# A hybrid decoder block on one core: the z and x projections get the stationary operand swapped

## The reference

```python
def reference(x, ...):                       # x: (1, 256, 2048) float32
    hn = rmsnorm(x, norm_mix_w)
    z, xbc, dt_raw, u, g_a, g_b = split(hn @ w_in)
    xbc = silu(causal_dwconv(xbc, conv_a_w, conv_a_b))     # 4 taps; x: 3072 channels, b and c: 1024 each
    y_a = mamba2(z, xbc, dt_raw) @ w_proj_a                # uses silu(z)
    y_b = s5(u)                                            # 64 groups, complex states
    h = x + (sigmoid(g_a) * y_a + sigmoid(g_b) * y_b) @ w_out
    h = h + conv_glu_ffn(rmsnorm(h))
    return rmsnorm(h)
```

## Time and profile before

| | us |
|---|---|
| runs | 1680.24, 1680.87, 1680.90 |
| median | 1680.87 |
| the profiled execution, its own time | 1680.3 |
| span of that execution | 1678.6 |

### The profile page before, as it was taken

The page is one execution under the profiler, slowest core; times in us unless marked ns, Lnnn a source line. Parts: engine busy times, 40 slices in busy tenths (PEclk is TensorE's granted clock), DMA queues, the critical chain, the costliest instruction groups (busy, mean ns, idle before and its releaser), DMA issues.

```text
span 1678.6 us, 24422 instructions
## 1 busy us (share of the span) xinstructions
PE 1667.1 (99%) x8340; PEld 1395.1 (83%) x8340; DVE 1320.3 (79%) x1685; ACT 962.7 (57%) x1271; POOL 216.4 (13%) x310
## 2 busy tenths in 40 slices
PE   9999999999999999999999999999999999999997
PEld 8888888888788888888888888888888888888886
DVE  7999999999998986545775868888878888845555
ACT  7676676766666667444557755444444444454553
POOL 7843342221000000000000200000000000000001
PEclk9999999999999999999999999999999999999999
DMA  7666766666666566656786577777777777666653
GB/s 254 213 197 199 204 206 200 193 188 190 194 217 231 191 219 189 199 191 201 239 254 232 174 233 241 243 241 244 242 244 241 245 232 248 225 194 195 191 189 123
DMA packets 174569, 358.49 MB, mean 214 GB/s; under 512 B 16880, under 2 KB 39584, under 8 KB 174368
## 3 DMA queue, kind: packets, MB, share of 16 engines
q1 hardware_dynamic: 162528, 338.26, 62.5%
q0 software_dynamic: 11248, 18.37, 4.6%
q10 hardware_dynamic: 720, 0.93, 0.2%
HBM read 335.41 MB, written 15.80 MB: 209 GB/s over the span
## 4 chain that ended last, share of the span: by engine, by line
PE 73%; DVE 2%; issue 0%; ACT 0%; DVEq 0%
PE psum L1822 22%; PE psum L1823 22%; PE psum L1824 22%; PE psum L1783 3%; PE psum L1785 2%; PE psum L1908 1%; DVE wlo L1107 0%; PE psum L1909 0%; DVE vn L1749 0%; PE psum L1933 0%; DVE bc L1303 0%; PE psum L1829 0%; PE psum L1924 0%; DVE dec L1416 0%; PE psum L1982 0%; PE psum L1979 0%
## 5 line engine op out<-in xcount | busy, mean ns | idle before, releaser
L1107 DVE TENSOR_TENSOR wlo<-raw,whi 128x1024 fp32r<-128x1024 f32 x580 | 709.6, 1230 | 321.3 <-ACT whi L666 314.0
L666 ACT ACTIVATE whi<-raw 128x1024 fp32r<-128x1024 f32 x580 | 611.9, 1058 | 577.1 <-PE psum L1824 455.1
L1783 PE MATMUL psum<-act,whi 128*128 128x512 f32 x1088 | 342.5, 396 | 0.0
L1822 PE MATMUL psum<-whi,nw 128*128 128x512 f32 x704 | 274.1, 389 | 0.0
L1824 PE MATMUL psum<-whi,nw 128*128 128x512 f32 x704 | 273.9, 389 | 0.0
L1823 PE MATMUL psum<-wlo,nw 128*128 128x512 f32 x704 | 273.9, 389 | 0.0
L1785 PEld LDWEIGHTS psum<-act,wlo 128*128 128x128 f32 x1088 | 204.4, 188 | 48.3
L1785 PE MATMUL psum<-act,wlo 128*128 128x256 f32 x1088 | 213.7, 278 | 0.0
L1783 PEld LDWEIGHTS psum<-act,whi 128*128 128x128 f32 x1088 | 165.6, 189 | 3.3 <-issue 2.8
L1824 PEld LDWEIGHTS psum<-whi,nw 128*128 128x128 f32 x704 | 132.1, 188 | 27.6
L1822 PEld LDWEIGHTS psum<-whi,nw 128*128 128x128 f32 x704 | 132.1, 188 | 27.3
(11 more groups left out here) (251 smaller groups left out, 2300.3 us busy)
## 6 DMA issues: line engine op xcount, KB each, us to landing
raw<-in_w_up SPq DMA_DIRECT2D x176, 512.0 KB, 4.9
raw<-in_w_zx SPq DMA_DIRECT2D x96, 512.0 KB, 3.7
raw<-in_w_down SPq DMA_DIRECT2D x88, 512.0 KB, 3.8
raw<-in_w_gate SPq DMA_DIRECT2D x64, 512.0 KB, 5.6
raw<-in_w_proj SPq DMA_DIRECT2D x48, 512.0 KB, 4.4
raw<-in_w_bc SPq DMA_DIRECT2D x32, 512.0 KB, 3.7
raw<-in_w_glu SPq DMA_DIRECT2D x32, 512.0 KB, 4.4
raw<-in_w_out SPq DMA_DIRECT2D x32, 512.0 KB, 4.8
```

The source lines that it names most:

```text
L666: fn(whi[:, s, :], raw[:, s, :], ACTF.Copy).then_inc(hi_ready, 1)
L1107: V.tensor_tensor(wlo[:, s, :], raw[:, s, :], whi[:, s, :], ALU.subtract).then_inc(lo_ready, 1)
L1783: mm(psum[:, b + t, :], whi[:, s, cols(t)], x, start=first, stop=False)
L1822: mm(banks[:, t, :], x_hi, high[:, k], start=j == 0 and k == 0, stop=False)
```

## The change

For zx, PE now calls `unit_tokens`: a chunk is 8 units and gives 256 channels of z and 256 of x for all 256 tokens; a turn has two chunks. Weights are loaded with 2 KB pieces in place of 4 KB ones, from the same data. `take_hsum` and `add_halves` are gone for zx. In their place ACT copies a finished chunk to `flat_x` (`zx_blocks`, two instructions, at the start of rounds 0 and 2), SP writes it to DRAM in four DMAs (`zx_write`, behind the load of unit 2 or 10 of the next turn), waits for them and reads it back into `quad_x` (`zx_fetch`, behind the load of unit 3 or 11), and DVE turns it (`zx_turned_back`, four instructions of 128x256, near the end of rounds 1 and 3): two for z into `zblk`, two for x into `cpad`. So x's tap, convolution and silu follow a chunk later than before: chunk 2i at r = 0 of turn i+1, chunk 2i+1 at r = 2. The last two chunks, 10 and 11, are convolved in bc0, next to bc0's own groups; chunk 11 goes through a pad of its own (`last_pad`).

The core of the diff:

```diff
@@ SyncE
+            def zx_write(c):
+                sp.wait_ge(zx_free, c + 1)
+                for q in range(4):
+                    sp.dma_start(blocks_at[:, :, q, :].rearrange("j p x -> p j x"),
+                                 flat_x[32 * q:32 * q + 32, :, :, :, :].rearrange("p j s t b -> p j (s t b)")
+                                 ).then_inc(zx_written, 16)
+            def zx_fetch(c):
+                sp.wait_ge(zx_written, c * 64 + 64)
+                sp.dma_start(quad_x[:, :, :, :, :].rearrange("p q s t b -> p (q s t b)"),
+                             blocks_at.rearrange("j p q x -> (j p) (q x)")).then_inc(zx_read, 16)
+            def zx_moves(turn, j):
+                if j % 8 == 2:
+                    zx_write(turn * 2 + (j // 8 - 2))
+                if j % 8 == 3:
+                    zx_fetch(turn * 2 + (j // 8 - 2))
@@ ScalarE
+            def zx_blocks(c, cc):
+                act.wait_ge(unit_used, c * 8 + (UNIT0["zx"] + 8))
+                if not (isinstance(c, int) and c == 0):
+                    act.wait_ge(zx_written, c * 64)
+                for t in range(2):
+                    ins = fn(flat_x[:, :, :, t, :].rearrange("p j s b -> p s j b"),
+                             chunk_banks("zx", cc)[:, t, :].rearrange("p (s j b) -> p s j b", s=4, j=4), ACTF.Copy)
+                ins.then_inc(zx_free, 1)
...
+            def z_silu(c):
+                fn(zx[:, ds(c * 2, 2), 0, :], zblk[:, :, :], ACTF.Silu).then_inc(z_done, 1)
@@ VectorE
-                elif name == "zx" and r % 2 == 0:
-                    add_halves(zx[:, ds(i * 4 + r, 2), 0, :], g0 + r, i * per)
...
+            def zx_turned_back(c):
+                pad = cpad
+                dve.wait_ge(zx_read, c * 16 + 16)
+                if isinstance(c, int) and c == 11:
+                    pad = last_pad
+                    V.memset(pad[:, :, 0:3], 0.0).then_inc(pad_zeros, 1)
+                if not (isinstance(c, int) and c == 0):
+                    dve.wait_ge(z_done, c)
+                for t in range(2):
+                    V.transpose(zblk[:, :, t * P:t * P + P].rearrange("p s (q b) -> p q s b", q=4),
+                                quad_x[:, :, 0:2, t, :])
+                if not (isinstance(c, int) and c == 0):
+                    dve.wait_ge(x_conv, c)
+                for t in range(2):
+                    ins = V.transpose(pad[:, :, 3 + t * P:3 + t * P + P].rearrange("p s (q b) -> p q s b", q=4),
+                                      quad_x[:, :, 2:4, t, :])
+                ins.then_inc(zx_turned, 1)
@@ VectorE, mixer_turn
-                    if r or start:
+                    if before[0] == "u" or name == "bc" and r:
                         group_sums(*before)
...
-                    group_conv(*before)
+                    if before[0] != "zx":
+                        group_conv(*before)
+                    if chunks and not start and r % 2 == 0:
+                        x_conv_pair(blk * 2 + (r // 2 - 2))
                     s5_scan(tile, last)
...
-                    if r == per - 1 and not last:
+                    if name == "bc" and r == per - 1 and not last:
                         group_sums(name, i, r)
...
                         last_state_sum(blk)
+                    if r == 3 and name == "zx" or r == 1 and chunks and not start:
+                        zx_turned_back(blk * 2 + (r // 2 - 1))
                     lo(3)
@@ TensorE
+            def zx_turn(i, prev):
+                for c in range(2):
+                    for j in range(8):
+                        if prev is None and c == 0:
+                            pe.wait_ge(vlo_ready, j // 2 + 1)
+                        if prev is not None and c == 1 and j == 0:
+                            pe.wait_ge(y5_out, prev + 1)
+                        unit_tokens("zx", c, j, act16, i)
+                        if c == 0 and j == (0 if prev is None else 1):
+                            s5_drive(i, prev is None)
+                            if prev is not None:
+                                pe.wait_ge(zx_free, i * 2)
+                                s5_products(prev, YS5)
```

More of the change, by code:

```diff
@@ L353, in _, with zx_units @@
                     sp.dma_start(craw[:, :, :, :], a["s5_c"]).then_inc(c_in, 16)
+                if name == "zx":
+                    w = a["w_zx"].rearrange("(c g q) p (h n) -> c q h p g n", g=2, q=quads, h=2)
+                    def zx_units(i):
+                        for j in range(4 * quads):
+                            n, c, q, half = UNIT0[name] + j, j // (2 * quads), j % (2 * quads) // 2, j % 2
+                            sp.wait_ge(lo_ready, i * (4 * quads) + (n - RING + 1))
+                            sp.dma_start(raw[:, n % RING, :].rearrange("p (g n) -> p g n", g=2),
+                                         w[ds(i * 2 + c, 1), q, half].rearrange("o p g n -> (o p) g n")
+                                         ).then_inc(w_in[n % RING], 16)
+                            if not (isinstance(i, int) and i == 0):
+                                zx_moves(i, j)
+                    zx_units(0)
+                    with sp.Fori(1, groups // 4) as i:
+                        zx_units(i)
+                    continue
+                if name == "bc":
+                    for j in range(groups * quads):
+                        n = UNIT0[name] + j
+                        sp.wait_ge(lo_ready, n - RING + 1)
+                        sp.dma_start(raw[:, n % RING, :], a["w_bc"][j]).then_inc(w_in[n % RING], 16)
+                        if j < 16:
+                            zx_moves(6, j)
+                    continue
                 if name == "up":
@@ L762, in sines, with group_tap @@
                    bias=TWO_PI / 4).then_inc(tab_ready, 1)
[L764 to L768, removed]
+            def group_tap(i, r):
+                _, per, quads, u0, g0 = phase("bc")
                 act.wait_ge(sum_ready, i * per + (g0 + r + 1))
@@ L771, in group_tap @@
                 for t in range(2):
[L772 to L775, removed]
+                    to, q = bc[:, ds(i * 4 + r, 1), t, :], i * 8 + (24 + 2 * r + t)
                     ins = fn(to.rearrange("p o n -> p (o n)"), cpad[:, t, 3:3 + L], ACTF.Identity,
@@ L778, in group_tap, with group_silu @@
                 ins.then_inc(tap_ready, 1)
[L780 to L797, removed]
+            def group_silu(i, r):
+                act.wait_ge(conv_done, i * 4 + (r + 1))
+                to = bc[:, ds(i * 4 + r, 1), :, :].rearrange("p o c n -> p (o c) n")
+                fn(to, to, ACTF.Silu).then_inc(xbc_done, 1)
@@ new lines, in zx_blocks, with x_first_tap @@
+            def zx_blocks(c, cc):
[6 more added lines that the diff above has]
+                ins.then_inc(zx_free, 1)
+            def x_first_tap(c):
+                act.wait_ge(zx_turned, c + 1)
+                act.nop(nofuse=True)
+                pad = last_pad if isinstance(c, int) and c == 11 else cpad
+                for t in range(2):
+                    q = c * 2 + t
+                    ins = fn(zx[:, ds(q, 1), 1, :].rearrange("p o n -> p (o n)"), pad[:, t, 3:3 + L], ACTF.Identity,
+                             scale=col("conv_a_w", q * 4 + 3), bias=col("conv_a_b", q))
+                ins.then_inc(x_tap, 1)
@@ L799, in mixer_turn, with x_silu @@
+            def x_silu(c):
+                act.wait_ge(x_conv, c + 1)
+                act.nop(nofuse=True)
+                to = zx[:, ds(c * 2, 2), 1, :]
+                fn(to, to, ACTF.Silu).then_inc(xbc_done, 1)
+            def z_silu(c):
+                fn(zx[:, ds(c * 2, 2), 0, :], zblk[:, :, :], ACTF.Silu).then_inc(z_done, 1)
             def mixer_turn(name, i, blk, prev):
                 _, per, quads, u0, g0 = phase(name)
-                start = prev[0] == "u"
+                first, chunks = prev[0] == "u", name == "zx" or i == 0
@@ L806, in mixer_turn @@
                     before = (name, i, r - 1) if r else prev
+                    behind = blk * 2 + (r // 2 - 2)
                     last = name == "bc" and i == 1 and r == per - 1
-                    group_hsum(*before)
+                    if before[0] != "zx":
+                        group_hsum(*before)
+                    elif r % 2 == 0:
+                        zx_blocks(blk * 2 + (r // 2 - 1), 1 - r // 2)
                     hi(0)
-                    if r >= 2 or not start:
+                    if r >= 2 or not first:
                         act.wait_ge(x5_ready, blk * 4 + (r - 1))
@@ L813, in mixer_turn @@
                     hi(1)
-                    group_tap(*before)
+                    if before[0] == "bc":
+                        group_tap(*before[1:])
+                    if chunks and not first and r % 2 == 0:
+                        x_first_tap(behind)
                     if not last:
@@ L818, in mixer_turn @@
                     hi(2)
-                    group_silu(*before)
+                    if before[0] == "bc":
```

(58 more changed lines are left out.)

16 lines of the change are left out of this document (13 added, 3 removed).

## The result

The changed kernel takes 1699.44 us (median of 1697.13 to 1700.22), the one before 1680.74 beside it: ratio 1.011, 95% interval 1.0092 to 1.0127. It is 18.7 us slower where the forecast was 0.4 us faster, 1680.5 us, and the upper end of its range 1687.0. The profiled execution took 1700.2 us (span 1698.6), so differences read from its trace add up to 20.0 us.

The account below looks back on a forecast made before the run. TensorE bounds the kernel to bc0's drive, VectorE from there to the first gate turn. By VectorE alone, -1.05 - 6.9 + 1.8 + 3.9 + 1.9 = -0.4 us: 1680.5 us, range 1677.0 to 1687.0.

Parts of the forecast that it names:

- What bounds the kernel: Two chains: TensorE until the drive of bc0, then VectorE from there to the first gate turn.
- the first chain: Up to the drive of bc0, TensorE's own work sets the time, 46.86 us a turn before the change.
- TensorE in zx, -6.0 us: Zx phase: 12 matmuls a unit instead of 16 save 0.062 us on each of 96 units, 6.0 us less.
- The spacing rule: Matmuls in zx: columns/2.4 ns plus 2.5 ns each; by it the phase would gain 1.0 us instead of 6.0.
- ScalarE's two copies ... nothing: Zx turns: two copies of a chunk replace four equal-sized copies of half sums, ACT idling a third of a turn; no cost.
- VectorE in t1 to t5, +0.4 a turn: Four sums removed (2.4 us), eight transposes added (2.8 us) a turn; 229.3 us of work against TensorE's 229.4.
- The lead at unit 14 of t2: VectorE's thinnest lead over TensorE, 1.7 us before, falls to 0.7 us and holds.
- The round trip, 1.9 us: Before the transposes in t1 to t5, VectorE waits for chunk data coming back from DRAM, 1.9 us in sum.
- the held load, "late by 0.2 at most": SP's fetch holds back the load of unit 12 or 20; its split starts at 13.8 against VectorE's 13.6 us.
- The rival that named this: Round trips dominate at the wait for `zx_read` and the held load: 1.0 us at eight moves, +5.7, 1686.6; chance 0.25.
- Loads in 2 KB pieces: In SP's queue, a load in 2 KB pieces takes 4.9 us to land; counted for the load behind the fetch.
- bc0, +3.9 us: In bc0 VectorE gets one more convolution (2.4 us), four transposes (1.4) and a memset (0.1): 3.9 us more, all showing.

Follow-up runs that it names:

- e8: As e3, but zx loads come in 4 KB rows, z and x from wrongly ordered weights; 1677.84 us, ratio 0.9984.
- e9: As e3, with zx weights laid out in DRAM in loading order, 4 KB rows, whole block computed; 1677.73 us, ratio 0.9984.
- e1: Changed kernel plus a one-column silu in round 2 of t0, so no table load is left in the loop; 1691.81 us, ratio 1.007.
- e2: Changed kernel with the chunk's DRAM write issued two units sooner, behind unit 0 or 8; table loads stay; 1691.90 us, ratio 1.0067.
- e3: Changed kernel with both edits, the added silu in t0 and the write two units sooner; 1681.49 us, ratio 1.0004.
- e4: As e1, but the fetch reads weights instead of the chunk, before SP waits for the writes; next load still held; 1686.95 us, ratio 1.0039.
- e5: As e3, with VectorE's six instructions of chunk 11's convolution left out of bc0; 1679.40 us, ratio 0.999.
- e6: As e5, with chunk 10's convolution in bc0 left out too; 1677.27 us, ratio 0.998.

## Why the prediction was wrong, point by point

**What bounds the kernel**: right for the kernel before, e8 and e9, where TensorE has no wait in zx and its waits in bc are for VectorE. In the changed kernel TensorE waits 13.8 us in zx, so there the first chain runs through the engines that feed it.

**TensorE in zx, -6.0 us**: right in size. e9's t1 to t4 are 1.04 us shorter each than before (0.99 forecast) and its drive of bc0 comes at 336.84 against 343.26, 6.4 us sooner. The spacing rule of the Trainium skill ("TensorE: Matmul & The Clock Gate", "Back-to-back issue gap") would have left 1.0 us of it. That section gives the rule for an isolated matmul, and this stream, at 0.227 us a matmul of 512 columns, does not follow it.

**"ScalarE's two copies ... nothing"**: the step that failed first. The copies were counted, the functions were not: taking silu out of t0 changes which table stands when the loop begins, and 15 loads of 1.28 us follow. They cost 7.0 us (e1) or 10.4 with the moves early (e2 against e3). The row that could have warned is the single table load of the kernel before between 60 and 448 us, in t0, at the silu that the change moves. The Trainium skill ("ScalarE: Activation LUTs", "What ACT_TABLE_LOAD costs") gives 1283 ns for the load and about as much again for a drain. The trace agrees with the former, 1.28 us; of a drain it shows nothing here, since the load starts at 206.06, 0.02 us after the instruction before it, and the next one at 207.36, 0.02 us after the load's end.

**VectorE in t1 to t5, +0.4 a turn, "just no slack left"**: right, and it is why everything else counted. With a budget equal to TensorE's to 0.1 us, no wait has anywhere to hide. The lead at unit 14 of t2 held too: neither e9 nor the changed kernel waits there. The 3.9 us that the changed kernel loses in t2 are at unit 6, where VectorE comes late by the waits for the round trip and for the table, both at other steps of the prediction.

**The round trip, 1.9 us, and the held load, "late by 0.2 at most"**: the mechanism was named, the terms were mis-sized. VectorE waited 9.8 us for the data, where 1.9 was forecast. Late data and held load together cost 10.3 us with the tables repaired (e1 against e3), roughly half each (e4), and 7.0 with the tables as they were (e2). The working took the trip and the load's landing from up, where the medians are 3.9 and 4.9 us, and set them against VectorE's order as if nothing else were late. In zx the fetch lands in 4.9 us (up to 6.3) and a load in up to 8.6, with POOL's DMAs in flight beside it. A median against a margin of 0.2 us is a coin toss at each of eleven moves, and each loss stays, since the budget has no slack. The prediction quoted a fit of the Trainium skill ("DMA: Bandwidth & Descriptors", "Anatomy of one DMA") for software-generated DMAs, by which the trip would be shorter still; the page of the profile lists the queue that moves 350.85 of 371.09 MB, SP's, as hardware_dynamic, so the fit was no yardstick for this trip. The rival that named this had the right place and sign, at 6 us: too small, since it priced only the trip.

**Loads in 2 KB pieces**: the prediction used their slower landing once, for the held load. That every load of the phase is affected was left out: 3.9 us (e3 against e8), or 3.8 with the layout made right (e9).

**bc0, +3.9 us**: right in mechanism (e5, e6) and near in size. Beyond the drive of bc0 the changed kernel loses 6.3 us (20.0 - 13.7), but e9 only 4.5 (from 6.4 to 1.9 ahead in span), and one convolution is worth 2.7 us (e5). The two in one round add a stall of their own, 3.2 us in e3 and 1.5 in e9; how much of that the chain would have taken anyway is not separated.

The 18.7 us, then, with the edits taken in this order: tables 7.0 (e1), the moves' place 10.3 (e1 against e3), rows of 4 KB 3.8 (e9 against e3), which leaves -2.5. The two terms of the forecast that held come to -2.1: TensorE's -6.0 and bc0's +3.9. In another order the parts would be of other size; the sum is what is measured.

## What to carry to other kernels

When two engines' budgets in a loop are equal to a tenth of a microsecond, waits that would hide elsewhere add up at full price; give every transfer in the loop a lead of whole units, not of a median's remainder. A change that moves a function from before a loop into it, or out of the pass that precedes it, must be read for the table that stands at the loop's entry. A fetch that waits for a write in the queue that feeds the ring holds the ring: issue the write as soon as its data is there (7.0 us here by itself, 10.3 with the tables repaired).

## What the runs showed of the hardware

After TensorE's wait of 3.9 us in t2 its granted clock was 0.50 for the next 3.6 us, the 1.2 GHz level, and the matmuls of 512 columns came 0.43 us apart where they come 0.23 apart otherwise. They did so until 177.7 us: 12 matmuls took 5.3 us where they take 2.7 otherwise. Windows of the changed kernel around that wait:

```profile
168.00:172.40 4.40, 0.58 (x3) 0.16 (x1) 4.40 (x7) 2.71 (x3) 2.68 (x4) 0.85 0.07 25
172.40:176.00 3.60, 3.56 (x8) 2.82 (x9) 3.60 (x4) 3.21 (x7) 1.85 (x2) 0.50 0.55 166
```

So t2 is 7.5 us longer than forecast with 4.6 us of waits in it, and the clock accounts for 2.6 of the rest. The waits of up to 1.6 us in t3 to t5 left the clock at 1.00. The length of a wait did not settle it alone: in bc0 the clock was 0.50 in the 3.6 us after a wait of 3.14 us in e2, and 1.00 after one of 3.16 us in e3.
